# Filling a sparse gate matrix: one-hot matmuls against indirect 4-byte DMAs with add

## What is computed

```python
def peer_ffn(xn, wq, sub_keys, u, v):
    q = (xt @ wq).reshape(t, 8, 2, 128)
    sc = jnp.einsum('thpc,hpnc->thpn', q, sub_keys)
    top_v, top_i = lax.top_k(sc, 16)
    cand_v = (top_v[:, :, 0, :, None] + top_v[:, :, 1, None, :]).reshape(t, 8, 256)
    cand_id = (top_i[:, :, 0, :, None] * 128 + top_i[:, :, 1, None, :]).reshape(t, 8, 256)
    best_v, best_pos = lax.top_k(cand_v, 16)
    expert = jnp.take_along_axis(cand_id, best_pos, axis=-1)
    gate = jax.nn.softmax(best_v, axis=-1)
    # out[c] = sum over 8 heads, 16 ranks of gate * gelu(x[c] . u[expert]) * v[expert]
```

## Time and profile before

| | |
|---|---|
| median of three runs | 3367.11 us |
| the profiled execution | 3371.16 us |
| its span | 3369.2 us |
| mean granted TensorE clock | 0.987 of full speed |
| busy: TensorE / VectorE / ScalarE / GpSimd | 3222.2 / 2468.4 / 1112.5 / 615.2 us |
| queries and spilled units | about 632 to 905 us of the span |
| lone units and gate matrix | about 905 to 1245 us |
| dense groups | about 1245 to 3020 us |

### The profile page before, as it was taken

How to read it: one execution, slowest core, us unless ns; L and a number is a source line. 1 busy time by engine, 2 the same in 40 slices (tenths; PEclk the granted TensorE clock), 3 DMA queues, 4 the chain that set the end, 5 groups by cost and what they waited for, 6 DMA issues and landing times.

```text
span 3369.2 us, 47672 instructions
## 1 busy us (share of the span) xinstructions
PE 3222.2 (96%) x17333; PEld 2998.7 (89%) x17333; DVE 2468.4 (73%) x3432; ACT 1112.5 (33%) x1411; POOL 615.2 (18%) x405
## 2 busy tenths in 40 slices
PE   7999999999987878999999999999999999999997
PEld 5777788898977778999999999999999999999785
DVE  6444443699978877888878787887888888885645
ACT  4224332222234443333233333333333333323432
POOL 2120000011145541121111111121121112110200
PEclk9999999999989999999999999999999999999998
DMA  4231122333355558887878888787887878773222
GB/s 144 84 120 47 53 88 99 105 109 110 120 180 209 209 211 283 279 303 271 289 281 287 288 284 295 265 300 269 284 288 282 297 277 297 273 256 119 90 98 100
DMA packets 230384, 694.36 MB, mean 206 GB/s; under 512 B 17328, under 2 KB 75184, under 8 KB 194864
## 3 DMA queue, kind: packets, MB, share of 16 engines
q1 hardware_dynamic: 188848, 418.77, 36.1%
q0 software_dynamic: 36864, 268.45, 22.1%
q10 hardware_dynamic: 4608, 6.29, 0.5%
HBM read 657.79 MB, written 35.65 MB: 206 GB/s over the span
## 4 chain that ended last, share of the span: by engine, by line
PE 43%; DMA 7%; DVE 7%; issue 3%; ACT 2%; DVEq 0%; SPq 0%; ACTq 0%
PE bank L477 14%; PE bank L479 14%; PE bank L478 14%; DMA raw<-in_u_t 5%; DMA raw<-in_v 3%; DVE w_lo L1193 3%; ACT w_hi L867 2%; DVE row_acc L1506 1%; DVE row L1499 1%; DVE h L1622 1%; DVE x_lo L1634 1%; DVE h_a L1563 0%; DVE h_s L1557 0%; ACT h_g L1094 0%; DVE proj L1705 0%
## 5 line engine op out<-in xcount | busy, mean ns | idle before, releaser
L477 PE MATMUL bank<-x_hi,w_hi 128*128 128x384 f32 (+1 forms) x3024 | 1082.0, 358 | 37.4 <-DVE x_lo L1210 18.6
L478 PE MATMUL bank<-x_lo,w_hi 128*128 128x384 f32 (+1 forms) x3024 | 1070.2, 354 | 0.0
L479 PE MATMUL bank<-x_hi,w_lo 128*128 128x384 f32 (+1 forms) x3024 | 1069.6, 354 | 0.0
L867 ACT ACTIVATE w_hi<-raw 128x1024 fp32r<-128x1024 f32 (+1 forms) x668 | 689.8, 1050 | 910.0 <-DMA raw<-in_v 341.2
L1193 DVE TENSOR_TENSOR w_lo<-raw,w_hi 128x1024 fp32r<-128x1024 f32 (+1 forms) x662 | 807.1, 1236 | 246.1 <-ACT w_hi L867 236.4
L477 PE MATMUL bank<-a_hi,w_hi 128*128 128x384 f32 x2048 | 688.1, 336 | 18.5 <-DVE w_lo L1193 15.4
L478 PE MATMUL bank<-a_lo,w_hi 128*128 128x384 f32 x2048 | 685.4, 335 | 0.0
L479 PE MATMUL bank<-a_hi,w_lo 128*128 128x384 f32 x2048 | 685.4, 335 | 0.0
L477 PEld LDWEIGHTS bank<-x_hi,w_hi 128*128 128x128 f32 x3024 | 571.8, 189 | 87.8 <-DVE w_lo L1193 21.9
L479 PEld LDWEIGHTS bank<-x_hi,w_lo 128*128 128x128 f32 x3024 | 571.5, 189 | 39.1
L478 PEld LDWEIGHTS bank<-x_lo,w_hi 128*128 128x128 f32 x3024 | 572.0, 189 | 38.4 <-issue 1.2
(11 more groups left out here) (194 smaller groups left out, 2237.5 us busy)
## 6 DMA issues: line engine op xcount, KB each, us to landing
raw<-in_u_t SPq DMA_DIRECT2D x256, 512.0 KB
raw<-in_v SPq DMA_DIRECT2D x256, 512.0 KB
gate_matrix<-g_blk SPq DMA_DIRECT2D x12, 2048.0 KB, 6.3
g_tile<-gate_matrix SPq DMA_DIRECT2D x32, 768.0 KB, 9.4
raw<-in_w_o SPq DMA_DIRECT2D x32, 512.0 KB
raw<-in_w_q SPq DMA_DIRECT2D x32, 512.0 KB
raw<-in_w_gate SPq DMA_DIRECT2D x32, 512.0 KB
raw<-in_w_in SPq DMA_DIRECT2D x26, 512.0 KB
```

The lines of the kernel that those rows point to most:

```text
L477: pe.matmul(out, w_hi[slot][:, blk, :], m_hi, start=first, stop=False)
L478: pe.matmul(out, w_hi[slot][:, blk, :], m_lo, start=False, stop=False)
L479: return pe.matmul(out, w_lo[slot][:, blk, :], m_hi, start=False, stop=last)
L867: act.activation(w_hi[slot][:, 8 * s:8 * s + n, :], raw[s][:, 0:n, :], ACT.Copy)\
```

## The change

- The gate matrix lies in DRAM as one list of cells, `(expert, token)` in 16384 x 384, with expert = first key x 128 + second key. It is cleared by 24 stores of 1 MB from a zero tile (SP, in the attention heads' and the output projection's loops).
- VectorE does GpSimd's multiplies of `keys`, and computes for each head the expert numbers and the cell numbers (`pair_e`, `cell`), and the gates into `gates_all`.
- GpSimd writes each head's gates by 48 indirect DMAs (3 token blocks x 16 ranks), each of 128 single floats, with add: `put_gates`. Before a head's first one it waits until all of the heads before have landed.
- For the last head the puts come after the gathers of rows 0 to 3, and a row gather stands behind each four puts. After the last put has landed, GpSimd itself loads `g_tile` for groups 0 and 1 (`g_first`).
- The one-hots, their matmuls, evictions, the transposes of `sel` and the stores by block are gone; so are GpSimd's three `w_lo`. The 18 spilled units behind the last head (ALONE = 18) run one after the other, VectorE's `lo` of each followed by one row dot from the seventh on.

```diff
-ALONE = 7
-ALONE_POOL = 3
-U_BLOCK = U_ALONE + ALONE
+ALONE = N_GROUPS - 2 * (PH - 1)
...
+PUTS = TCD * TOPK
+N_ZERO = 24
...
-EARLY = ALONE - ALONE_POOL + N_TB
+EARLY = 16
...
-        g_dram = nc.dram_tensor("gate_matrix", (N_TB, P, NK, TB), F32, kind="Internal").ap()
+        g_cells = nc.dram_tensor("gate_matrix", (NK * NK * TD, 1), F32, kind="Internal").ap()
+        g_zero = g_cells.rearrange("(n p c) a -> n p (c a)", n=N_ZERO, p=P)
+        g_groups = g_cells.rearrange("(g i j t) a -> g j i (t a)", g=N_GROUPS, i=GROUP, j=P)
...
+        zeros = x_rows
...
# SP
+            sp.wait_ge(zeros_made, 1)
+
+            def clear(n):
+                sp.dma_start(g_zero[n], zeros[:, :]).then_inc(zeros_stored, 16)
+
             with sp.Fori(2, HEADS) as n:
                 load_unit(n + U_HEAD, head_w(n))
-            with sp.Fori(0, DC) as n:
+                clear(n - 2)
+            with sp.Fori(0, N_ZERO - HEADS + 2) as n:
+                load_unit(n + U_WO, packed(w_o, n))
+                clear(n + HEADS - 2)
...
-            for n in range(ALONE + 2):
-                load_unit(U_ALONE + n, packed(u_t, spilled(2 * (PH - 1) + n)))
...
+            with sp.Fori(0, ALONE) as n:
+                load_unit(n + U_ALONE, packed(u_t, spilled(n + 2 * (PH - 1))))
...
# TensorE
-            for e in range(1, ALONE_POOL + 1):
-                alone(e)
...
-                mm.then_inc(hk_turned, 1)
-            for e in range(ALONE_POOL + 1, ALONE):
-                alone(e)
...
+            alone(1, 1)
+            with pe.Fori(1, ALONE // 2) as e2:
+                for k in range(2):
+                    alone(2 * e2 + k, k)
...
-            unit_dense(U_PEER, U_PEER % 2, 0, quarter_done=groups(N_TB - 1))
+            unit_dense(U_PEER, U_PEER % 2, 0)
...
# VectorE, for each head
+                dve.wait_ge(pick_ready, 2 * hd + 2)
+                for p in range(2):
+                    ins = dve.tensor_tensor(
+                        picked[p][:, :, :].rearrange("p (t k) m -> p t k m", t=TC),
+                        pick[p][:, :, :].rearrange("p (t k) m -> p t k m", t=TC),
+                        t_if[p][:, :, :].unsqueeze(2).to_broadcast([P, TC, TOPK, TOPK]), ALU.mult)
+                step(ins)
...
+                step(dve.scalar_tensor_tensor(pair_e[:, :, :], pair[0][:, :, :], float(NK), pair[1][:, :, :],
+                                              ALU.mult, ALU.add))
+                dve.tensor_copy(expert_of_head(), pair_e[:, TCD, :])
+                step(dve.scalar_tensor_tensor(of_head(cell), pair_e[:, 0:TCD, :], float(TD),
+                                              rope_c[:, 2:2 + TCD].unsqueeze(2).to_broadcast([P, TCD, TOPK]),
+                                              ALU.mult, ALU.add))
...
             step, k = step_by_step(PER_TOPK * (PH - 1))
+            lo(U_ALONE + 1, (U_ALONE + 1) % 2)
             half_topk(step, 2 * PH - 2, 0)
+            lo(U_ALONE + 2, U_ALONE % 2)
             half_topk(step, 2 * PH - 1, 1)
+            lo(U_ALONE + 3, (U_ALONE + 1) % 2)
             best_pairs(step)
+            lo(U_ALONE + 4, U_ALONE % 2)
             keys_and_gates(step, PH - 1)
...
+            lo(U_ALONE + 5, (U_ALONE + 1) % 2)
...
             dve.wait_ge(rows_out, 4)
...
+            for k in range(EARLY - 2):
+                lo(U_ALONE + 6 + k, (U_ALONE + k) % 2)
+                row_dot(k, k % 4, row_loads(k))
+            for k in range(EARLY - 2, EARLY):
+                row_dot(k, k % 4, row_loads(k))
...
# GpSimd
+            def put_gates(hd, t, k):
+
+                if t == 0 and k == 0:
+                    pool.wait_ge(topk_step, PER_TOPK * (hd + 1))
+                    if hd:
+                        pool.wait_ge(gates_put, 16 * PUTS * hd)
+                pool.indirect_dma_start(g_cells, bass.IndirectOffsetOnAxis(ap=cell[:, t, hd, k:k + 1], axis=0),
+                                        gates_all[:, t, hd, k:k + 1], None, compute_op=ALU.add).then_inc(gates_put, 16)
...
+            pool.wait_ge(zeros_stored, 16 * N_ZERO)
+            for hd in range(PH - 1):
+                for t in range(TCD):
+                    for k in range(TOPK):
+                        put_gates(hd, t, k)
+            pool.wait_ge(topk_step, PER_TOPK * PH)
             pool.wait_ge(rows_out, 4)
-            for k in range(6):
+            for k in range(4):
                 load_row(k)
...
+            for t in range(TCD):
+                for k in range(TOPK):
+                    put_gates(PH - 1, t, k)
+                    if k % 4 == 3 and t * 4 + k // 4 + 4 < EARLY:
+                        load_row(t * 4 + k // 4 + 4)
+            pool.wait_ge(gates_put, 16 * PUTS * PH)
+            for par in range(2):
+                pool.dma_start(g_tile[par][:, :, :], g_groups[par]).then_inc(g_first[par], 16)
             for k in range(EARLY, 2 * ROWS):
                 load_row(k)
```

More of the change, by code:

```diff
@@ L160, in build_block @@
         picked = [at(f"picked{i}", one + (34 + 4 * i) * K, [P, TC * TOPK, TOPK]) for i in range(2)]
-        sel = [at(f"sel{i}", one + (42 + 2 * i) * K, [P, TC, PH, TOPK]) for i in range(3)]
+        pair = [at(f"pair{i}", one + 42 * K + 256 * i, [P, TC, TOPK]) for i in range(2)]
+        pair_e = at("pair_e", one + 42 * K + 512, [P, TC, TOPK])
+        gates_all = at("gates_all", one + 59 * K, [P, TC, PH, TOPK])
+        cell = at("cell", one + 61 * K, [P, TCD, PH, TOPK], U32)
         t_v = [at(f"t_v{i}", one + 48 * K + 256 * i, [P, TC, TOPK]) for i in range(2)]
@@ L170, in build_block @@
         t_if = [at(f"t_if{i}", one + 53 * K + 256 * i, [P, TC, TOPK]) for i in range(2)]
[L172 to L178, removed]
+        h_out = at("h_out", one + 62 * K + 512, [P, TD])
         H = TD * 4
@@ L182, in build_block @@
         a_lo = [at(f"a_lo{i}", one + H * (5 + i), [P, TD], F32R) for i in range(5)]
-        g_tile = [at(f"g_tile{i}", one + (15 + 6 * i) * K, [P, N_TB, GROUP, TB]) for i in range(2)]
+        g_tile = [at(f"g_tile{i}", one + (15 + 6 * i) * K, [P, GROUP, TD]) for i in range(2)]
         h_s = at("h_s", one + 27 * K, [P, TD])
@@ L271, in build_block @@
         h_in = [sem(f"h_in{i}") for i in range(2)]
[L273 to L280, removed]
+        zeros_made, zeros_stored = sem("zeros_made"), sem("zeros_stored")
+        gates_put = sem("gates_put")
+        g_first = [sem(f"g_first{i}") for i in range(2)]
         g_in = [sem(f"g_in{i}") for i in range(2)]
@@ L336, in row_loads @@
         def row_loads(k):
-            return k // 2 + 1 if k < EARLY else (k - EARLY) // 4 + 1 + (EARLY // 2 if k % 4 < 2 else 0)
+            return k // 4 + 1
         def peer_unit(g, k):
@@ L721, in sparse_rows, with alone @@
                 mm.then_inc(rows_made, 1)
-            def alone(e):
-                spill(2 * (PH - 1) + e, e % 2, U_ALONE + e, (U_ALONE + e) % 2)
+            def alone(e, k):
+                spill(e + 2 * (PH - 1), k, e + U_ALONE, (U_ALONE + k) % 2)
             sparse_rows(0)
             sparse_rows(1)
-            alone(0)
+            alone(0, 0)
             sparse_rows(2)
@@ L1044, in rows_evict @@
                 act.activation(x_rows[:, 4 * P * i:4 * P * (i + 1)], bank[6 + i % 2][:, :], ACT.Copy).then_inc(rows_out, 1)
-            for e in range(ALONE):
+            act.wait_ge(zeros_stored, 16 * N_ZERO)
+            for e in range(4):
                 hi(U_ALONE + e + 1, (U_ALONE + e + 1) % 2)
@@ L1053, in _ @@
                     act.activation(rinv_col[:, :], bank[2][:, 0:2], ACT.Copy).then_inc(col_made, 1)
-                if e == ALONE_POOL - 1:
+                if e == 3:
                     gates(PH - 1)
                 spill(2 * (PH - 1) + e, e % 2, U_ALONE + e)
[L1057 to L1089, removed]
+            with act.Fori(2, ALONE // 2) as e2:
+                for k in range(2):
+                    hi(2 * e2 + k + U_ALONE + 1, (U_ALONE + k + 1) % 2)
+                    spill(2 * e2 + k + 2 * (PH - 1), k, 2 * e2 + k + U_ALONE)
+            hi(U_PEER + 1, (U_PEER + 1) % 2)
             def gelu(j):
@@ L1442, in keys_and_gates @@
                        .then_inc(pick_ready, 1)
+                dve.wait_ge(pick_ready, 2 * hd + 2)
[5 more added lines that the diff above has]
+                step(ins)
+                for p in range(2):
+                    ins = dve.tensor_reduce(pair[p][:, :, :], picked[p][:, :, :].rearrange("p (t k) m -> p t k m", t=TC),
+                                            AX.X, ALU.add)
+                step(ins)
                 dve.wait_ge(gate_exp, hd + 1)
@@ L1561, in gate @@
                 dve.wait_ge(e_gelu, j + 1)
-                dve.wait_ge(g_in[par], 16 * n + 16)
-                dve.tensor_tensor(h_a[:, :].rearrange("p (b t) -> p b t", t=TB),
-                                  h_g[:, :].rearrange("p (b t) -> p b t", t=TB), g_tile[par][:, :, m, :], ALU.mult)\
+                if isinstance(n, int) and n == 0:
+                    dve.wait_ge(g_first[par], 16)
+                else:
```

(35 more changed lines are left out.)

155 lines of the change are left out of this document (29 added, 126 removed).

## The result

The changed kernel takes **3666.67 us** (median of 4 runs, 3664.78 to 3670.98) against 3369.09 for the kernel before (4 runs, 3363.27 to 3371.43): a ratio of **1.0888**, interval 1.0869 to 1.0907. The forecast was 3457, with a range of 3310 to 3620. The sign was right, the size was not: +298 us in place of +90, outside the range.

A forecast was written before the change was run, and what follows sets the result against it. The prediction took TensorE as busy except between queries and dense groups (304 of 382 us), where GpSimd's 384 puts would delay the second product 90 us: 3371.2 + 90 = 3461, less 4 gives 3457 us; range 3310 to 3620.

The forecast's parts named there:

- The mechanism: After the queries: GpSimd falls behind from the first head; VectorE stops in `row_dot(0)` about 966, then TensorE after seven units.
- twelve units behind it: Dense units after row 0 arrives, at 8.33 us each: 100 us.
- The wait between heads: On GpSimd, each head waits until the previous head's puts have landed: 3 us.
- The zeros' 24 stores: 1 MB stores on SP's queue during heads and output projection: costed at nothing; without cover at most 182 us in all.
- the put's price: Each of 384 indirect DMAs on GpSimd: 1.18 us, pitch 1.48 alone and 1.70 beside VectorE.
- R: Time when GpSimd issues the gather of row 0, behind seven heads of puts: 1224.
- the second product: Start of the first second product of group 0, ending the middle stretch: 1377, 90 us later than 1287.
- VectorE's part: Its operations delay GpSimd's DMA starts: 0.22 us per DMA beside the queries, about 0.5 us in the last head.
- The sum: Profiled execution 3371.2 plus 90 is 3461, less 4 to the median: 3457 us.
- Puts cheaper than 0.92 us: Rival on GpSimd: puts cheaper than a gather make the kernel faster, 3302 us at 0.70; chance 0.24, hidden puts 0.06.
- Pacing by the landing: Rival: each put must land before the next, pitch 2.4 + 0.3, 3847 us; chance 0.17 together with dearer puts.
- The chances: Forecast 0.46, dearer or landing-paced 0.17, within 0.2% 0.07, cheaper 0.24, hidden 0.06; faster 0.30, slower 0.63.

The follow-up runs named there:

- e5_plain_again: Second run of the changed kernel with its puts writing without the add: 3413.44 us, ratio 1.0142 against the kernel before the change.

## Why the prediction was wrong, step by step

**The mechanism held.** GpSimd falls behind from the first head; VectorE stops in `row_dot(0)` and TensorE with it after seven lone units, at 974.35 (forecast about 975); one long PE wait, released through `w_lo` by the `row` transfer; twelve units behind it in 110 us (100); nothing before 672 moved. The wait between heads is 2.1 to 2.8 us (3). The zeros' 24 stores, costed at nothing, cost nothing: the first cells are ready at 670.5, before at 672.4, and TensorE is busy 606 us up to 632, before 603.

**The step that failed is the put's price**: "three halves of it is 1.41, and I take the middle between 0.94 and that, 1.18 us". No run shows the 1.18, nor the three halves of a gather behind it: a put measured 1.55, between the gather's 0.94 and the 1.88 that the prediction kept as twice a gather. A put without the add is a gather's equal (0.96), the add brings 0.6 us; what in the add takes them is not shown. The middle between 0.94 and 1.41 was the author's estimate, without a row for the add. The price hits 384 times:

- a head beside a working VectorE: 106 to 110 us per 48 puts, 2.21 to 2.29 each, forecast 1.70;
- a head with VectorE idle: 1.98 to 2.02 each, forecast 1.48.

With 1.55 in place of 1.18 the prediction's own steps give R = 1342, the second product at 1513 and 3593 us. So this term is 136 of the 210 us by which the forecast missed, and alone it would have left the time inside the range.

**The step that was missing** is the gaps, of which no row before had one: 64 us, all before row 0. With them the mean pitch, VectorE idle, is 2.0 and not 1.86. They move R from 1342 to about 1406; it came at 1394.7, since VectorE and the waits between heads cost a little less than forecast.

**VectorE's part was right in kind.** From 632 to 905 a put takes 1.72 us in the mean, with VectorE idle 1.55: 0.17 us, forecast 0.22. In the last head, beside row dots of 2.3 us, the mean is 1.94: 0.39 us, forecast 0.5. It is spread unevenly: the longest (3.2 to 3.37 us) are four of the last head, the median of all 384 is 1.55.

**The sum, with measured terms.** Row 0 was forecast at 1224 and came at 1394.7: 171 us of the 192 by which the second product is later than forecast (1568.87 against 1377). From there it took 174 us, forecast 153. That this is close to the 171 which the steps give for a put of 1.55 us is luck, because two parts were off in opposite directions. The last put came at R + 129, where the steps say 139 for such a put. Behind it passed 45 us, where 32 were summed along the wrong path. The sum went over the landing of the puts and `g_tile`. That tile was there by about 1538, the first gating started at 1552.5, and VectorE waited for it nowhere. It waited for row 15, the last gather, issued behind the last put; its dot stands before the first eviction of group 0, for which TensorE waits. The rows, VectorE's and then TensorE's:

```profile
1531.75 2.29 DVE L1434 SCALAR_TENSOR_TENSOR row<-row,x_rows 128x2048 f32<-128x2048 f32 x1 [7.39 <-DMA row<-in_u_rows,expert]
...
1538.86 0.55 DVE L1461 TENSOR_TENSOR h_s<-bank,rinv 128x384 f32<-128x384 f32 x1
...
1539.46 0.69 PE L462 MATMUL bank<-x_hi,w_hi 128*128 128x384 f32 x1 [25.58 <-DVE h_s L1461]
```

The prediction had followed the rows only as far as row 11. With e5_plain_again the same steps can be read near the other end of the range. At a gather's price they gave row 0 at 1149 and the second product at 1294; measured 1169 and 1321, with 25 us of gaps that had no step.

**The rivals.** Puts cheaper than 0.92 us: no run shows one; the plain put is 0.96. Pacing by the landing (3847 us): no, puts follow each other after 1.86 us, while the last put of each of heads 0 to 5 has landed only 3.6 to 4.3 us after its start (head 0's starts at 778.86, and GpSimd's wait for it ends at 782.62).

**The chances** put 0.46 on puts of 0.96 to 1.45 us and 0.17 on everything dearer. With no row for the add, a price of 1.5 to 1.9 deserved more than that, and the upper end of the range should have been the one for 1.88 us, 3716.

Not tried: several offsets per partition in one DMA, which would make fewer puts, at a price that no run shows; and heads without the wait between them, since two heads' adds may meet in one cell.

## What to carry to other kernels

Before work moves to an engine that looks idle, multiply: the number of instructions times their pitch, against the period in which the producer delivers. Here 48 puts of some 2 us stood against 41.6 us a head, and the engine went from 18% busy to the only one that works; 16 of them fit, stay hidden in all heads but the last, and leave a gain of 1.5%. An operation for which the trace has no row should be priced by its ends, and where it does one thing more per element (here an add), from the dear end first.

## What the hardware showed that was not expected

- **An indirect DMA with add costs GpSimd 1.55 us per 128 elements, without add 0.96** (medians of 384 each), and its elements become packets of their own: 92,544 on the queue against 49,536. The adds also keep the DMA engines busier: in the stretch with nothing but puts their share is 0.20, without the add 0.02 (e5_plain_again), for under 1 GB/s either way.
- **GpSimd has idle gaps at a spacing that follows `dynamic_dma_scratch_size`**, 1.8 to 5 us each time in the changed kernel: every 7 and 14, 15 and 28, 18 and 35 puts for 2048, 4096 and 5120 bytes. From 2048 to 5120 bytes the kernel gains 70 us (3712.9 to 3643.0, one execution each).
- Small transfers beside the query stage raised the DMA share from 0.33 to 0.48 (to 0.34 without the add) without costing TensorE any of its 273 us.
